# Block 1's mixer: the P·V products of both query halves of a head pair in one place, in the next pair's third step

## The reference

```python
h = rmsnorm(x, mix_norm[l]); proj = h @ w_in[l]        # 256 pooled + q, k, v of 12 heads of 64
y_pool = multiscale_pool(v_pool, pool_w[l], pool_scale[l])
q, k = apply_partial_rope(q, cos, sin), apply_partial_rope(k, cos, sin)
# three dilated windows (128,1), (512,4), (2048,16), mixed by their softmax denominators:
num = sum(wts[i][..., None] * branches[i][0] for i in range(3))     # P.V of each branch
den = sum(wts[i] * branches[i][2] for i in range(3))
x = x + concatenate([y_pool, (num / den[..., None])], -1) @ w_out[l]
```

## Time and profile before

| | |
|---|---|
| median of 3 runs (lowest, highest) | 2559.98 us (2558.35, 2560.38) |
| the profiled execution's own time | 2559.84 us |
| its span, first to last instruction | 2557.7 us |
| PE busy | 2518.2 us, 98% of the span |
| PEld / DVE / ACT / POOL busy | 80% / 51% / 22% / 59% |
| mean granted clock of PE | 0.996 |
| chain that ended last: PE / DVE / ACT / POOL | 96% / 2% / 1% / 1% |
| the matmuls of `values`, L755 (two buffers) | 384, in 24 calls |
| PE idle before `values` | 22 times for "issue" (3.7 us in all), twice for ACT (0.8 us) |
| the mixer's steps in layer 1 / layer 2 | from about 403 to 566 us / 1354 to 1517 us |

### The profile page before, as it was taken

One profiled execution on the slowest core, in us unless ns is written; L12 is line 12 of the kernel. 1 busy time (PEld: TensorE's weight loads), 2 busy tenths in 40 slices (PEclk: granted clock), 3 DMA queues, 4 the chain that ended last, 5 costly groups with the idle time before them and its releaser, 6 DMA issues.

```text
span 2557.7 us, 33017 instructions
## 1 busy us (share of the span) xinstructions
PE 2518.2 (98%) x11986; PEld 2058.2 (80%) x11986; DVE 1315.8 (51%) x1556; ACT 566.9 (22%) x1033; POOL 1519.2 (59%) x858
## 2 busy tenths in 40 slices
PE   8999999999999999999999999999999988999998
PEld 6888888778888888888888778888887776888887
DVE  5555527656555315556137656555226656655522
ACT  2110014652111001110015552111013564111000
POOL 5666666436666666666665536666664322666664
PEclk9999999999999999999999999999999999999999
DMA  4233222113222322332322112332233111332232
GB/s 166 96 98 98 94 96 75 58 42 98 93 96 98 99 93 97 98 95 93 99 96 69 56 50 93 98 121 93 98 99 132 57 35 34 99 96 93 99 99 74
DMA packets 66149, 228.67 MB, mean 89 GB/s; under 512 B 8721, under 2 KB 11665, under 8 KB 65681
## 3 DMA queue, kind: packets, MB, share of 16 engines
q1 hardware_dynamic: 64352, 225.67, 27.1%
q10 hardware_dynamic: 1712, 1.82, 0.2%
HBM read 225.36 MB, written 2.10 MB: 89 GB/s over the span
## 4 chain that ended last, share of the span: by engine, by line
PE 96%; DVE 2%; ACT 1%; POOL 1%; issue 1%; DMA 0%; SPq 0%; DVEq 0%; POOLq 0%; ACTq 0%
PE bank L606 28%; PE bank L608 28%; PE bank L607 28%; PE bank L623 2%; PE bank L755 2%; PE bank L740 2%; PE bank L724 1%; PE bank L629 1%; PE bank L725 1%; PE bank L978 1%; PE bank L993 1%; DMA raw<-in_stream 0%; POOL wl L570 0%; PE bank L614 0%; PE bank L970 0%
## 5 line engine op out<-in xcount | busy, mean ns | idle before, releaser
L570 POOL TENSOR_TENSOR wl<-raw,wh 128x1024 fp32r<-128x1024 f32 x412 | 1035.7, 2514 | 34.5
L567 POOL TENSOR_SCALAR wh<-raw 128x1024 fp32r<-128x1024 f32 x412 | 445.5, 1081 | 985.8 <-PE bank L608 947.8
L606 PE MATMUL bank<-xh,wh 128*128 128x512 f32 x2096 | 818.8, 391 | 0.2 <-POOL wl L570 0.2
L607 PE MATMUL bank<-xl,wh 128*128 128x512 f32 x2096 | 816.4, 389 | 0.0
L608 PE MATMUL bank<-xh,wl 128*128 128x512 f32 x2096 | 816.2, 389 | 0.0
L608 PEld LDWEIGHTS bank<-xh,wl 128*128 128x128 f32 x2096 | 393.5, 188 | 83.0
L607 PEld LDWEIGHTS bank<-xl,wh 128*128 128x128 f32 x2096 | 393.6, 188 | 81.4 <-issue 0.2
L606 PEld LDWEIGHTS bank<-xh,wh 128*128 128x128 f32 x2096 | 393.7, 188 | 81.1 <-POOL wl L570 0.6
L606 PE MATMUL bank<-acth,wh 128*128 128x512 f32 (+1 forms) x902 | 346.4, 384 | 0.0
L607 PE MATMUL bank<-actl,wh 128*128 128x512 f32 (+1 forms) x902 | 346.2, 384 | 0.0
L608 PE MATMUL bank<-acth,wl 128*128 128x512 f32 (+1 forms) x902 | 346.2, 384 | 0.0
(11 more groups left out here) (269 smaller groups left out, 2344.0 us busy)
## 6 DMA issues: line engine op xcount, KB each, us to landing
raw<-in_stream SPq DMA_DIRECT2D x412, 512.0 KB, 3.7
x<-in_x SPq DMA_DIRECT2D x4, 512.0 KB, 7.9
w1k<-in_w1k SPq DMA_DIRECT2D x1, 2048.0 KB, 9.0
w1v_low<-in_w1v SPq DMA_DIRECT2D x1, 1024.0 KB, 6.8
w1v_high<-in_w1v SPq DMA_DIRECT2D x1, 1024.0 KB, 10.0
out_dram<-x SPq DMA_DIRECT2D x4, 256.0 KB, 2.6
out_dram<-x SPq DMA_DIRECT2D x1, 768.0 KB, 3.7
invcount<-in_c_invcount ACTq DMA_DIRECT2D x1, 512.0 KB, 6.1
```

The costliest lines, as they stand in the source:

```text
L567: nc.gpsimd.tensor_scalar(wh[:, h, :, :], src, 1.0, 1.0, ALU.mult, ALU.mult)\
L570: nc.gpsimd.tensor_tensor(wl[:, h, :, :], src, wh[:, h, :, :].bitcast(F32), ALU.subtract).then_inc(split_done, 1)
L606: mm = nc.tensor.matmul(bank, wh[:, slot, k, :], rh, start=start, stop=False)
L607: mm = nc.tensor.matmul(bank, wh[:, slot, k, :], rl, start=False, stop=False)
```

## The change

`values` of the first half (2j) moves from step 6 of its pair to step 2 of the next one, and there both halves run one after the other, ahead of that step's turn and no longer behind it. The first half's wait for copies is raised to that of the second half, so that the second half's own wait is already met. The last pair keeps its two calls where they were. That makes 5 moves in each of the two layers. Instructions are neither added nor taken away.

```diff
-                    pe.wait_ge(pte_done, l * STEPS + (4 * h + 6))
+                    pe.wait_ge(pte_done, l * STEPS + (4 * (h if j == PAIRS - 1 else 2 * j + 1) + 6))
...
                             pe.wait_ge(proj_read, l * U_PROJ + 5)
+                        if s == 2 and j > 0:
+                            values(2 * j - 2)
+                            values(2 * j - 1)
                         if g >= 2:
                             turn(g - 2)
-                        if s == 2 and j > 0:
-                            values(2 * j - 1)
                         if s == 3 and j > 0:
                             reciprocal_rows(j - 1)
-                        if s == 6:
+                        if s == 6 and j == PAIRS - 1:
                             values(2 * j)
```

## The result

The changed kernel takes 2576.37 us (median of 4 runs, 2573.98 to 2576.99) against 2559.89 for the kernel before: the ratio is 1.0062, 95% interval 1.0050 to 1.0073. It is 16.5 us slower; 14.3 were forecast, and the time lies in the range given. The profiled execution took 2576.63 us, its span is 2574.4.

A forecast was written before the change was run, and what follows sets the result against it. PE was taken as the bound, 98% busy. Per layer 0.5 (pair 0), 2.6 (pairs 1 to 3) and 4.1 (last pair), twice, made 14.4 us: 2574.3 us, 0.56% slower, range 2566 to 2580.

The forecast's parts named there:

- What PE spends: PE in steps 2 and 6: step 2 grows by 1.69 us, step 6 shrinks by 2.05; a move gives back 0.36.
- fourth rival: Between the two values calls in step 2: the seam costs a whole switch, 0.36 x 10 more, 2578 us; chance 7%.
- PE's busy time down by little: Sign named for a right forecast: on the profile, PE's busy time falls slightly while the span rises by 14 us.
- third rival: Steps 6 and 7: POOL's L567 starts before low_q's second half, holding low_q and both low_k; +9 us, 2583; chance 7%.
- first rival: DVE's low_k isn't held by POOL in the new places; only the last pair waits: +2.2 us, 2562.2; chance 8%.
- The middle pairs: Pairs 1 to 3: second low_k, held by POOL's L570, makes step 1's scores wait 1.23 us; balance +0.87 each.
- Pair 0: First pair of each layer: less of the wait is new; +0.5 us taken, between -0.36 and +0.87.
- The last pair: Thin cover, without fill: waits before scores, value_turn and reciprocal_rows, both calls ahead of the turn; balance +4.1 us.
- from there on the engines keep their distances: Last pair, from reciprocal_rows in step 3 on: PE, DVE and ACT keep their distances, so no further delay arises.
- The sum: Both layers: 2 x (0.5 + 2.6 + 4.1) = 14.4 us on the profiled 2559.84.
- second rival: Ten moves: only PE's saved switches count and every wait stays covered; -3.6 us, 2556.4; chance 4%.
- Each microsecond in the mixer is one of the end: PE bounds the feed-forwards and output projection around the mixer too, so mixer time counts fully at the end.

The follow-up runs named there:

- e4_inner_gate: Changed kernel with the move for pairs 0 to 3 only, and POOL waiting for both low_k in those pairs: 2556.53 us, ratio 0.9983 to the kernel before.
- e1_gate: Changed kernel plus one POOL wait per pair, ahead of L567, until both low_k are done: 2560.97 us, ratio 1.0003 to the kernel before.
- e8_gate_low: Changed kernel plus a POOL wait for both low_k placed between L567 and L570: 2563.50 us, ratio 1.0011 to the kernel before.
- e2_inner: Changed kernel with the move made for pairs 0 to 3 only, pair 4 keeping its old order: 2567.70 us, ratio 1.0026 to the kernel before.
- e7_rows_late: Changed kernel with the last pair's reciprocal_rows in step 4 instead of step 3: 2573.84 us, ratio 1.0048 to the kernel before.
- e3_last: Changed kernel with the move made only for pair 4 into the last pair: 2568.80 us, ratio 1.0038 to the kernel before.
- e6_turn_first: Changed kernel with both values calls behind step 2's turn, not ahead of it: 2572.91 us, ratio 1.0044 to the kernel before.
- e5: Kernel before, nothing moved, with only POOL's wait for both low_k added: 2560.04 us, ratio 0.9999 to the kernel before.

## Why the prediction was right, step by step

- **What PE spends.** Step 2 grows by 1.70 (1.69), step 6 shrinks by 2.05; the seam is 0.21 (0.22), and the fourth rival, a switch at the seam, is out. A move gives 0.35 to 0.40 (0.36). Most of the 0.04 beyond it: the second scores matmul starts 0.34 behind the first when P·V stands in front, 0.31 when a turn does. One sign named in the forecast did not come, "PE's busy time down by little": on the page it is up by 3.0, and in the mixers it is unchanged. Where nobody waits the saved switches do show, as 3.2 us less of it in the mixers of e4_inner_gate; here the part of each wait that the view counts as busy, 0.25 of the 1.26 above, makes up for them.
- **POOL first or DVE first.** L567 started 0.09 us behind low_q's second half in pair 1 and in the last pair (542.83 against 542.74). The order held in every place, by 0.09 us where 0.11 was forecast, and the third rival didn't occur. The first rival fell with the 1.43 and 2.17 us of low_k, and e1_gate and e8_gate_low show that POOL makes them; its time, 2562.2, is about what e1_gate has, which is that case made on purpose.
- **The middle pairs.** Wait of 1.26 (1.23), balance +0.88 (+0.87), and 6.28 alone in e2_inner (6.2).
- **Pair 0.** +0.5 was a guess between two ends, not worked out; that it is +0.53 in the ledger is luck. There the second low_k lasts 2.5 us behind L570.
- **The last pair.** +4.2 (+4.1): step 0 +2.08 (2.07), step 1 another 0.52 (0.53), value_turn 0.74 (0.73), the two calls 1.70, reciprocal_rows 1.22 (1.1). The path from the turn to vtok's end was 2.48 rather than 2.41. The sentence that from there on the engines keep their distances was right by luck: e7_rows_late shows pool_low at 0 to 0.1 us of slack.
- **The sum.** 14.65 in the mixers (14.4). The time moved by 16.5, and the 1.9 between lie outside the mixers. No term of the sum has them. "Each microsecond in the mixer is one of the end" holds until 2072 us of the kernel before (PE's starts there are as late as at layer 2's last scores, to 0.04) and not through the rest of block 2.
- **The other side.** The second rival, -3.6 with ten moves, needs both POOL's wait and the last pair left alone; e4_inner_gate has it with eight: -3.2 in the mixers.

## What to carry to other kernels

Work that is taken out of the bounding engine's order at one place was also the cover of whatever another engine does meanwhile: list who must be done in the stretch that comes earlier, and with how much room. An engine that is released earlier by the same step (POOL here) moves too, and may land on a stretch of DVE where each holds the other; look in the trace for a place where the same two instructions already meet, it gives the price. If they meet, one wait on the engine with time to spare may be worth more than the edit.

## What the runs showed of the hardware

**Holding each other.** A DVE instruction with two SBUF inputs that starts beside a running POOL instruction ends 0.53 to 0.57 us behind POOL's end. Those seen here take 0.69 alone, and took 1.4 to 1.5 behind L567 and 2.17 to 2.78 behind L570. With DVE first, L567 takes 1.4 to 1.5 for 1.06 and L570 2.7 to 2.9 for 2.4 (2.9 in e8_gate_low). t and v_out, which have an input in a bank, stayed within 0.69 beside both (v_out in rows 8, with L570 in flight from 543.39 to 546.10).

**The clock behind a wait**, which I had not expected. In e8_gate_low PE waits 1.86 and 1.85 us at the last pair's start. Stretches behind it, layer 1 then layer 2 (last columns: granted clock, DMA share, GB/s):

```profile
540.80:544.20 3.40, 3.40 (x12) 2.66 (x11) 2.65 (x7) 0.81 (x2) 2.54 (x1) 0.51 0.00 0
...
1495.00:1498.40 3.40, 3.40 (x22) 2.84 (x21) 3.00 (x8) 1.71 (x5) 2.89 (x1) 1.00 0.00 0
```

In layer 1 the clock is granted at half, 1.2 GHz, for 3.4 us right behind the wait, and the matmuls last 0.63 us for 0.39:

```profile
540.30 0.50 PE L736 MATMUL bank<-ks,qs 128*128 128x512 f32 x1 [1.86 <-DVE kl L1710]
540.64 0.45 PE L737 MATMUL bank<-kl,qs 128*128 128x512 f32 x1
540.89 0.63 PE L618 MATMUL bank<-mh,wh 128*128 128x512 f32 x1
```

It costs 1.5 us there (step 0 to step 1 of the scores 3.85 for 2.32). Of the profiles with this wait e3_last, e7_rows_late, e6_turn_first and e8_gate_low show it in one layer of two, the changed kernel in none; behind the 1.1 us of e1_gate it never came. The layer with it is longer than the other by 0.35, 0.26, 0.42 and 1.6 us in this order. In the first three the waits for the second low_k and for v_out, which the other layer has, are gone from the list: the slower PE comes to them late enough. In e8_gate_low no such wait follows that could take it up. So the price of a wait of nearly 2 us has a part of 0.3 to 1.6 us that comes and goes.

**Block 2** has three to six such half-clock stretches of 3.4 us in every profile, the kernel before included (at 2074, 2098 and two in a row at 2105), among its own short waits. They fall in different places in each kernel, and the last one of the changed kernel, at 2175, falls on a stretch where PE is busy:

```profile
2175.00:2178.40 3.40, 3.08 (x7) 2.48 (x8) 0.95 (x2) 0.59 (x1) 0.00 (x0) 0.51 0.47 157
```

The same matmuls of PE, in the kernel before and then in the changed one:

```profile
2160.25 0.50 PE L606 MATMUL bank<-mh,wh 128*128 128x512 f32 x1 [1.78 <-DVE ml L2030]
...
2161.97 0.39 PE L607 MATMUL bank<-ml,wh 128*128 128x512 f32 x1
...
2175.32 0.79 PE L606 MATMUL bank<-mh,wh 128*128 128x512 f32 x1 [1.78 <-DVE ml L2031]
...
2178.47 0.40 PE L607 MATMUL bank<-ml,wh 128*128 128x512 f32 x1
```

Both stand behind a wait of 1.78 us, and from the first to the eighth it is 1.72 us before and 3.15 after: 1.43 of the changed kernel's 2.2 us arise in this one stretch. The others arise among the half-clock stretches from 2072 to 2122 (+0.5 in all, with up to 1.5 gained on the way) and at the very end (+0.2).

From the last scores of layer 2 to the end of the span the profiles gain or lose against the kernel before: after +2.2, e1 +0.8, e2 +2.2, e3 -1.5, e4 0.0, e5 +0.7, e6 +1.4, e7 -1.1, e8 -0.8. No order by the edit is in them, but the three that gain are the three with the fewest half-clock stretches in block 2 (three each; the others have four to six). So the traces show where most of the changed kernel's 2 us arise. Why a stretch falls there in this kernel and not in the one before stays open: no run changes that alone.
